# Second and third projections: the first 512 turned rows taken as 128 and 384, the weight asked for between them

## The reference, cut to what matters

```
def fox_shared_kv(x, c, kv_ada_w, kv_ada_b, w_kv, b_f, k_norm):
    shift, scale = ada_params(c, kv_ada_w, kv_ada_b, 2)
    u = rms_norm(x) * (1 + scale) + shift
    p = u @ w_kv
    k = rms_norm(p[..., :D_B].reshape(B, L, H_B, HD_B)) * k_norm
    v = p[..., D_B:2 * D_B].reshape(B, L, H_B, HD_B)
    logf = jax.nn.log_sigmoid((p[..., 2 * D_B:] + b_f).astype(jnp.float32))
...
    proj = h @ w_in                                   # fox_mixer, h made like u
    q = rms_norm(proj[..., :D_B].reshape(B, L, H_B, HD_B)) * q_norm * (HD_B ** -0.5)
    g = proj[..., D_B:]
```

## Time and profile before

| | us |
|---|---|
| median of three runs | 3133.67 |
| lowest and highest run | 3128.68, 3133.70 |
| profiled execution, its time | 3129.55 |
| its span on the core | 3128.0 |
| PE busy | 2843.9 |
| DVE busy | 1476.7 |
| ACT busy | 945.1 |
| POOL busy | 804.0 |

### The profile page before, as it was taken

The page is one execution under the profiler, slowest core; times in us unless marked ns, Lnnn a source line. Parts: engine busy times, 40 slices in busy tenths (PEclk is TensorE's granted clock), DMA queues, the critical chain, the costliest instruction groups (busy, mean ns, idle before and its releaser), DMA issues. The chain is left out here.

```text
span 3128.0 us, 41449 instructions
## 1 busy us (share of the span) xinstructions
PE 2843.9 (91%) x15730; PEld 2033.8 (65%) x15730; DVE 1476.7 (47%) x3562; ACT 945.1 (30%) x1547; POOL 804.0 (26%) x460
## 2 busy tenths in 40 slices
PE   5589999997899996999969999789999999994999
PEld 2367777776677874788758777455555555552767
DVE  1542222211787646641157015566666666653343
ACT  0322222211555654220033112134444444433000
POOL 1220000000000002000011000268887888786000
PEclk7589999999899998999989999789999999997999
DMA  9532222212566435211151331333313431313764
GB/s 337 196 89 81 54 85 81 78 48 87 178 209 218 155 98 200 78 59 67 49 177 48 78 72 50 101 109 100 88 57 106 116 93 37 112 34 134 245 204 133
DMA packets 281927, 355.20 MB, mean 114 GB/s; under 512 B 40044, under 2 KB 172460, under 8 KB 281681
## 3 DMA queue, kind: packets, MB, share of 16 engines
q1 hardware_dynamic: 279364, 344.23, 34.9%
q0 software_dynamic: 2304, 8.39, 0.7%
q10 hardware_dynamic: 72, 0.07, 0.0%
HBM read 250.28 MB, written 102.10 MB: 113 GB/s over the span
## 5 line engine op out<-in xcount | busy, mean ns | idle before, releaser
L2341 POOL TENSOR_TENSOR at_p_sum<-at_p_sum,at_p 128x1024 f32<-128x1024 f32 (+3 forms) x264 | 521.9, 1977 | 84.5 <-ACT at_p L2187 61.6
L2187 ACT ACTIVATE at_p<-psum 128x1024 f32<-128x1024 f32 (+1 forms) x320 | 270.3, 895 | 383.8 <-PE psum L2014 376.7
L2238 DVE CUSTOM_DVE_ANT_0 psum<-psum,at_f_wide 128x512 f32<-128x512 f32 (+3 forms) x640 | 377.0, 631 | 0.0
L672 POOL TENSOR_TENSOR kv_h_lo<-kv_aux,kv_h_hi 128x512 fp32r<-128x512 f32 x16 | 24.1, 1507 | 1059.6 <-ACT kv_h_hi L649 1028.7
L2094 PE MATMUL psum<-at_p,at_v 128*64 128x512 f32 (+3 forms) x1280 | 270.5, 544 | 0.7 <-ACT at_p L2187 0.7
L768 PE MATMUL psum<-kv_w_hi,kv_h_hi 128*128 128x512 f32 x512 | 201.3, 393 | 13.0 <-DVE kv_w_lo L964 13.0
L768 PE MATMUL psum<-gla_w_hi,gla_h_hi 128*128 128x512 f32 x512 | 201.4, 393 | 2.7 <-DVE gla_w_lo L964 2.7
L769 PE MATMUL psum<-kv_w_lo,kv_h_hi 128*128 128x512 f32 x512 | 200.3, 391 | 0.0
L770 PE MATMUL psum<-kv_w_hi,kv_h_lo 128*128 128x512 f32 x512 | 200.2, 391 | 0.0
L769 PE MATMUL psum<-gla_w_lo,gla_h_hi 128*128 128x512 f32 x512 | 199.4, 390 | 0.0
L770 PE MATMUL psum<-gla_w_hi,gla_h_lo 128*128 128x512 f32 x512 | 199.3, 389 | 0.0
(11 more groups left out here) (425 smaller groups left out, 6196.3 us busy)
## 6 DMA issues: line engine op xcount, KB each, us to landing
mod_w<-in_ada_w SPq DMA_DIRECT2D x12, 2048.0 KB, 18.1
at_f_wide<-F SPq DMA_DIRECT2D x32, 512.0 KB, 5.0
at_page<-in_cache_k SPq DMA_DIRECT2D x32, 512.0 KB, 3.6
gla_w_raw<-in_gla_w_in SPq DMA_DIRECT2D x6, 2048.0 KB, 7.7
mod_w<-in_kv_ada_w SPq DMA_DIRECT2D x4, 2048.0 KB, 9.7
v_gla<-gla_stage SPq DMA_DIRECT2D x32, 256.0 KB, 2.0
sg_gla<-gla_stage SPq DMA_DIRECT2D x32, 256.0 KB, 2.0
gl_sg<-sg_gla SPq DMA_DIRECT2D x16, 512.0 KB, 3.9
```

What stands on the lines that cost most here:

```text
L672: pool.tensor_tensor(part(h_lo, k, G), h_tmp[0], part(h_hi, k, G).bitcast(F32), ALU.subtract)\
L2187: act.activation(p_tile[e % PT][:, :, skip:NB], pair_of(bank_st[e % 2])[:, :, skip:NB], ACT.Exp)\
L2238: op = dve.tensor_tensor_reduce(pair_of(at(n))[:, a, 0:w], pair_of(at(n))[:, a, 0:w], f_wide[:, a, c * NB:c * NB + w], 1.0, -3.0e38, ALU.s ...
L2341: pool.tensor_tensor(p_sum[s][:, :, skip:NB], p_sum[s][:, :, skip:NB], p_tile[e % PT][:, :, skip:NB], ALU.add).then_inc(p_added, 1)
```

## The change

A table PARTS takes the place of the four parts of 512: rows 0 to 128, 128 to 512, and then the three parts of 512 as before. Whatever went over four parts goes over five: the semaphores, the loads on SP, ACT's and DVE's and POOL's operations, which are as wide as the part (128, 384 or 512). On SP the weight is still asked for after the first part, which is now the one of 128 rows. ACT and DVE do the parts 1 and 2 of the new table behind the weight's split, where they did part 1; the last two parts keep their places ahead of tiles 1 and 5. PE waits for the low halves at the tiles 0, 1, 4, 8 and 12.

```diff
+    PARTS = [(0, P), (P, NB)] + [(G * NB, (G + 1) * NB) for G in range(1, NG)]
...
-            part_loaded = [sem(f"part_loaded{G}") for G in range(NG)]
+            part_loaded = [sem(f"part_loaded{G}") for G in range(len(PARTS))]
...
-            part = lambda a, k, G: a[:, k, G * NB:(G + 1) * NB]
+            part = lambda a, k, G: a[:, k, PARTS[G][0]:PARTS[G][1]]
...
-            return {1: 2, 5: 3}.get(t) if turned_x is not None and p.base == 0 else None
+            return {1: 3, 5: 4}.get(t) if turned_x is not None and p.base == 0 else None
...
-                    dve.tensor_scalar(h_tmp[u], part(h_lo, k + u, G).bitcast(F32), modT[:, scale_block + k + u, 0:1],
+                    dve.tensor_scalar(h_tmp[u][:, 0:wide], part(h_lo, k + u, G).bitcast(F32), modT[:, scale_block + k + u, 0:1],
...
-                    for G in range(NG):
+                    for G, (begin, end) in enumerate(PARTS):
                         if G == 1:
                             load_w(plan[0], 0)
-                        sp.dma_start(h_lo[:, :, G * NB:(G + 1) * NB].bitcast(F32),
-                                     turned_x.rearrange("(k p) t -> p k t", p=P)[:, :, G * NB:(G + 1) * NB])\
+                        sp.dma_start(h_lo[:, :, begin:end].bitcast(F32),
+                                     turned_x.rearrange("(k p) t -> p k t", p=P)[:, :, begin:end])\
                             .then_inc(part_loaded[G], 16)
...
-                        if turned_x is not None and p.base == 0 and t % R == 0:
+                        if turned_x is not None and p.base == 0 and t * P in [begin for begin, _ in PARTS]:
                             for u in range(2):
-                                pe.wait_ge(part_lo[u], (t // R + 1) * K // 2)
+                                pe.wait_ge(part_lo[u], ([begin for begin, _ in PARTS].index(t * P) + 1) * K // 2)
...
                 if turned_x is not None:
                     part_high(act, 1)
+                    part_high(act, 2)
...
                 if turned_x is not None:
                     part_values(dve, 1)
+                    part_values(dve, 2)
...
-                    for G in range(NG):
+                    for G in range(len(PARTS)):
                         part_low(pool, G)
```

More of the change, by code:

```diff
@@ L652, in part_values @@
         def part_values(dve, G):
+            wide = PARTS[G][1] - PARTS[G][0]
             dve.wait_ge(part_loaded[G], 16)
@@ L662, in part_values @@
                 dve.wait_ge(part_hi, 2 * pairs_before + 2)
-                dve.tensor_tensor(part(h_lo, k + 1, G), h_tmp[1], part(h_hi, k + 1, G).bitcast(F32), ALU.subtract)\
+                dve.tensor_tensor(part(h_lo, k + 1, G), h_tmp[1][:, 0:wide], part(h_hi, k + 1, G).bitcast(F32), ALU.subtract)\
                    .then_inc(part_lo[1], 1)
         def part_low(pool, G):
+            wide = PARTS[G][1] - PARTS[G][0]
             for k in range(0, K, 2):
@@ L671, in part_low @@
                 pool.wait_ge(part_hi, 2 * pairs_before + 1)
-                pool.tensor_tensor(part(h_lo, k, G), h_tmp[0], part(h_hi, k, G).bitcast(F32), ALU.subtract)\
+                pool.tensor_tensor(part(h_lo, k, G), h_tmp[0][:, 0:wide], part(h_hi, k, G).bitcast(F32), ALU.subtract)\
                     .then_inc(part_lo[0], 1)
```

## The result

The changed kernel takes 3134.43 us (median of 20 runs, 3125.61 to 3139.59), the kernel before 3128.94 us in 20 runs (3123.51 to 3136.91).

The account below looks back on a forecast made before the run. PE, busy for 91% of the span, plus its waits was taken to bound the kernel. On a base of 3131.4 us, 1.9 us of later reduction and 4.2 us of clock loss gave 3137.5 us; 8 in 10 range 3130 to 3145.

Parts of the forecast that it names:

- That PE's early start ends in the wait for the copy: Both stages: PE starts nearly 8 us earlier in kv_, then loses it waiting some 6 us before the fold.
- D, the start of the reduction of tile 0: End of DVE's chain in each stage: 0.4 us later in kv_ and 1.5 us later in fox_, 1.9 us together.
- The weight: Start of each stage: it lands at 1202.6 in kv_ and 1612.6 in fox_, so DVE does not wait for it.
- rival 2: Small packets save no transfer time, the weight lands as late as before, DVE splits later: 3143.2 us, chance 0.12.
- The waits: PE's new waits in each stage: about 2 us before tile 1 and about 6 us before the fold.
- The clock: PE's clock halves in the fold and first 4.2 us of tile 2: 2.1 us lost per stage, 4.2 together.
- Rival 1: The clock stays up through the wait before the fold, only the later D counts: 3133.3 us, chance 0.15.
- That the clock falls: Wait before the fold: longer than the 5.0 us after which the clock fell once, so it falls to half.
- The sum: Both stages: 1.9 us from D plus 4.2 us from the clock, together 6.1 us later.
- Rival 3: The fold comes free earlier than D says; at most 3.7 + 2.7 us won: 3125.0 us, chance 0.06.
- what happens to tile 2 goes into the end one for one: Behind tile 2 PE has no wait of size, so its gain or loses there move the kernel's end equally.

Follow-up runs that it names:

- e1: Changed kernel with the second 512 part moved behind tile 0's evacuation on ACT and DVE: 3122.26 us, ratio 0.9975 to the kernel before.
- e3: Changed kernel with unread products on PE, 9 behind the sample's products and 20 ahead of the fold: 3135.46 us; run again unchanged, 3133.18 us.
- e2: Changed kernel with ACT's copy of the sample's parts moved ahead of its wait for tile 0's reduction: 3127.40 us, ratio 1.0002 to the kernel before.

## Why the prediction was right, step by step

- **That PE's early start ends in the wait for the copy** held in both stages: 7.9 and 7.6 us earlier at the start, tile 2 no earlier. e1 shows the cause: with one part moved behind the reduction the stages are 9.7 and 7.1 us shorter than in the changed kernel.
- **D, the start of the reduction of tile 0**, was forecast 0.4 and 1.5 us later, and is 0.29 and 0.69 (1641.04 less the 3.56 by which fox_ starts late is 1637.48, against 1636.79): 0.98 instead of 1.9. By the rows above a pair of 128 takes 0.97 us (1200.17 to 1204.07 is four) and one of 384 takes 2.06 (1208.89 to 1217.14), against 0.95 and 2.05 in the prediction. In fox_ the term was too large because the sample's work, which stands ahead, also came earlier: L1032 at 1613.42, less 3.56 is 1609.86, where it stood at 1610.81.
- **The weight** landed ahead of need: PE starts at 1204.39 without the offset, 1204.5 was forecast, so rival 2 did not come about. DVE does not wait for it in the rows above.
- **The waits** were mis-sized. In kv_ the first is 3.59 us where about 2.3 was worked out: I took over the 9.94 us that tile 0 and the sample's products took before, but here the clock rose 2.8 us after tile 0 began (0.66 in 1207 to 1208), where it had taken 5.2, so they took 8.87. In fox_ the first wait is 2.24. The second waits are 4.42 and 4.45 where some 6 were worked out. I counted tile 1 at the full clock (5.78 us); the clock fell at the first wait, and tile 1 took 7.30 and 7.28. In kv_ it ended at 1224.15 without the offset, 1.65 us later than the 1222.5 that was forecast, and this shortened the second wait.
- **The clock** is the term that was mis-sized: 4.2 us forecast, 5.64 measured (6.62 less 0.98). I counted the half clock's cost in tile 2 only, at 2.1 us per stage; what is left over for it is 1.91 and 2.04 (3.05 less 0.29 and 0.85; 3.57 less 0.69 and 0.84). The fold itself, which I put at the half clock too but did not count, adds 0.85 and 0.84. That the two stages are 5.1 us shorter in e3 and 5.9 in e3_again than in the changed kernel is near the 5.64. Rival 1, that the clock stays, fell with the row of 1228 to 1229.
- **That the clock falls** was right, but for a reason that did not hold, and this part was luck. I expected the fall because the wait before the fold, some 6 us, was longer than the 5.0 us after which the clock had fallen once. The waits were 4.42 and 4.45 us, shorter than that, and the clock fell at both. It fell also at waits of 3.59 and 2.24 us, and of 2.29 us in fox_ of e1, but not at the 3.05 us in kv_ of e1. So the length of the wait alone does not tell whether the clock falls; what decides is open here.
- **The sum** in the stages is 6.6 us against 6.1. The timed difference is 5.0 us by the ratio and 5.5 by the medians; its interval, 3.1 to 7.2 us, holds both. Part of the distance from 3137.5 to 3134.43 is the base: I took 3131.4, and 20 runs of the kernel before have 3128.94.
- Rival 3, the fold free earlier, is what e2 built: at most 6.4 us were worked out for it, and the two stages gained 0.9, since PE then waits for banks, the limit by which the prediction had bounded it. So it holds for a loss only that what happens to tile 2 goes into the end one for one: in e2 the fold came 4.1 us earlier in kv_ (1225.42 less the 1.21 by which that stage starts late, against 1228.28), and the stage is 0.8 us shorter.

## What to carry to other kernels

A bottleneck engine that starts earlier gains only if the next thing that it needs moves too: follow each helper engine's order to the first place where the bottleneck comes back to it. Here one part of 512 columns ahead of a reduction, and not the split itself, decided between 5 us lost and 7 us won (e1). And a long wait cut into pieces is not the same wait: each piece can cost the clock again. In the changed kernel only the last one, with nothing to hide it, made the stages longer.

## What the runs showed of the hardware that was not expected

- The clock's first fall in kv_ came with PE already at work again: PE stood for 3.59 us until 1217.36, and the granted clock is 0.96 in 1217 to 1218 and 0.50 in 1218 to 1219. A wait that has ended can still be paid for after it.
- The shorter of two waits can be the one at which the clock falls: 2.29 us in fox_ of e1, after which tile 1 took 7.22 us, against 3.05 us in kv_ of e1, after which it took 5.62.
- With 19 products in kv_ and 19 in fox_ that nothing reads, inside a wait, the kernel was some 3 to 4 us slower by the runs (1.0013, 1.0004 to 1.0021), and the stages that hold them were no longer. The cause stays open.
- The spread of the runs goes with the clock: over the 31 runs of the kernel before that stand beside e1, each 0.001 less of mean granted clock goes with 1.4 us more (a straight line through them). So single profiles are compared by stage here, not by span.
